# One 512-column product in place of two 256-column products in the down phases of a two-block model kernel

## What is computed

```python
# first block
h = rms_norm(x, ffn_norm_w)
x = x + (silu(h @ ffn_w_gate) * (h @ ffn_w_up)) @ ffn_w_down     # ffn_w_down: 5632 x 2048
x = rms_norm(x, final_norm_w)
# second block
h = h + mixed
h = h + conv_ffn(rms_norm_2(h, ffn_norm), ffn_w_up_2, conv_w, conv_b, ffn_w_down_2)   # ends in (...) @ w_down
return h
```

## Time and profile before

| | |
|---|---|
| median of 3 runs | 2572.27 us (2571.93, 2572.27, 2579.01) |
| profiled execution, span from first to last instruction | 2567.9 us |
| TensorE busy (matmul) | 2471.7 us, 96% of the span |
| VectorE busy | 1468.9 us, 57% |
| ScalarE busy | 1113.8 us, 43% |
| first down phase | about 1150 to 1391 us |
| second down phase | about 2320 to 2559 us |

### The profile page before, as it was taken

How to read it: one execution, slowest core, us unless ns; L and a number is a source line. 1 busy time by engine, 2 the same in 40 slices (tenths; PEclk the granted TensorE clock), 3 DMA queues, 4 the chain that set the end, 5 groups by cost and what they waited for, 6 DMA issues and landing times.

```text
span 2567.9 us, 58065 instructions
## 1 busy us (share of the span) xinstructions
PE 2471.7 (96%) x24757; PEld 2437.4 (95%) x24757; DVE 1468.9 (57%) x1657; ACT 1113.8 (43%) x1096; POOL 69.6 (3%) x70
## 2 busy tenths in 40 slices
PE   6999978989899999999998899999999999999999
PEld 6999968889899999999998899989899999999999
DVE  5457687674544544454445557674567676765444
ACT  4334434453444445443334444353455554544333
POOL 1000050001000000000100000000000000000000
PEclk8999989999999999999999999999999999999999
DMA  5555300126455555566663565535455555555664
GB/s 163 195 196 192 135 18 4 36 79 186 158 189 192 196 193 188 192 195 192 188 195 99 182 227 216 198 131 161 151 196 191 188 192 196 192 189 192 196 194 150
DMA packets 171475, 431.57 MB, mean 168 GB/s; under 512 B 17711, under 2 KB 23484, under 8 KB 170204
## 3 DMA queue, kind: packets, MB, share of 16 engines
q1 hardware_dynamic: 170123, 422.30, 50.0%
q10 hardware_dynamic: 1232, 7.52, 0.8%
HBM read 427.59 MB, written 2.17 MB: 167 GB/s over the span
## 4 chain that ended last, share of the span: by engine, by line
PE 89%; DVE 8%; ACT 2%; issue 1%; SPq 0%; DMA 0%; POOL 0%; DVEq 0%; ACTq 0%; POOLq 0%
PE ps L1813 27%; PE ps L1815 27%; PE ps L1814 27%; DVE LOW L984 1%; PE ps L1853 1%; ACT HIW L555 1%; DVE NSQ L1018 1%; PE ps L1959 1%; DVE H_ROWS L1026 0%; DVE TM L1237 0%; DVE LO L1241 0%; DVE TT L1238 0%; DVE CV L1271 0%; DVE rstd L1008 0%; DVE GT L1253 0%
## 5 line engine op out<-in xcount | busy, mean ns | idle before, releaser
L984 DVE TENSOR_TENSOR LOW<-RAW,HIW 128x2048 fp32r<-128x2048 f32 (+2 forms) x400 | 910.6, 2277 | 974.8 <-ACT HIW L555 974.8
L1813 PE MATMUL ps<-H_ROWS,HIW 128*128 128x256 f32 x4928 | 1369.6, 278 | 39.4 <-DVE LOW L984 16.9
L1814 PE MATMUL ps<-H_ROWS,HIW 128*128 128x256 f32 x4928 | 1368.6, 278 | 0.0
L1815 PE MATMUL ps<-H_ROWS,LOW 128*128 128x256 f32 x4928 | 1367.3, 277 | 0.0
L555 ACT ACTIVATE HIW<-RAW 128x2048 fp32r<-128x2048 f32 (+2 forms) x400 | 761.4, 1904 | 1178.8 <-PE ps L1815 1174.8
L1813 PEld LDWEIGHTS ps<-H_ROWS,HIW 128*128 128x128 f32 x4928 | 930.6, 189 | 43.1 <-issue 21.4
L1815 PEld LDWEIGHTS ps<-H_ROWS,LOW 128*128 128x128 f32 x4928 | 931.7, 189 | 0.0
L1814 PEld LDWEIGHTS ps<-H_ROWS,HIW 128*128 128x128 f32 x4928 | 930.5, 189 | 0.0
L1813 PE MATMUL ps<-HID,HIW 128*128 (+1 forms) x1408 | 388.7, 276 | 1.3 <-DVE LOW L984 1.3
L1815 PE MATMUL ps<-HID,LOW 128*128 (+1 forms) x1408 | 388.6, 276 | 0.0
L1814 PE MATMUL ps<-HID,HIW 128*128 (+1 forms) x1408 | 388.6, 276 | 0.0
(11 more groups left out here) (351 smaller groups left out, 1497.7 us busy)
## 6 DMA issues: line engine op xcount, KB each, us to landing
RAW<-in_ffn_w_up SPq DMA_DIRECT2D x264, 512.0 KB, 4.3
RAW<-in_ffn_w_down SPq DMA_DIRECT2D x176, 512.0 KB, 4.7
RAW<-in_w_in SPq DMA_DIRECT2D x96, 512.0 KB, 4.1
RAW<-in_fox_w_in SPq DMA_DIRECT2D x96, 512.0 KB, 4.4
RAW<-in_ffn_w_gate SPq DMA_DIRECT2D x88, 512.0 KB, 3.7
RAW<-in_w_out SPq DMA_DIRECT2D x32, 512.0 KB, 5.4
RAW<-in_fox_w_out SPq DMA_DIRECT2D x32, 512.0 KB, 4.7
INV<-rows_out ACTq DMA_DIRECT2D x4, 1024.0 KB, 7.0
```

The source lines that it names most:

```text
L984: V.tensor_tensor(LOW[:, u_const % 4, 0:n], RAW[:, u_const % 4, 0:n], HIW[:, u_const % 2, 0:n].bitcast(F32), ALU.subtract).then_inc(lo_mad ...
L1813: mm(o_, hi_w, h_hi, start=start, stop=False)
L1814: mm(o_, hi_w, h_lo, start=False, stop=False)
L1815: i = mm(o_, lo_w, h_hi, start=False, stop=stop)
```

## The change

In both down phases, and only there, the first two products of each (k, f) become one: the high weight block is loaded once and meets the 2 x 256 columns `HID[:, :, k, :]` (high part, then low part, 45,056 bytes apart in each partition), and the 512 result columns fill the whole bank `ps[f]`. The third product, low weight x high activation, is still added into columns 0 to 255. At the end of a half the two halves of each bank have to be added: `residual` first adds columns 256 to 511 to `X`, waits until that instruction has completed (`settle`), and then adds columns 0 to 255 and frees the bank. Nothing else changes; the orders of ScalarE, GpSimd and SyncE are the same.

```diff
-            def residual(m0, u_end, half):
+            def residual(m0, u_end, half, both=False):
                 for f in range(GROUP):
                     summed(m0, f, u_end)
                     x = X[:, half * 8 + f, :]
+                    if both:
+                        step(V.tensor_tensor(x, x, ps[f][:, T:2 * T], ALU.add))
+                        settle()
                     V.tensor_tensor(x, x, ps[f][:, 0:T], ALU.add).then_inc(bank_freed, 1)
...
             def down(u0, m0, last=False):
...
-                    residual(m0 + 7 * half, b + 22, half)
+                    residual(m0 + 7 * half, b + 22, half, both=True)
...
                         o_ = ps[f][:, 0:T]
-                        mm(o_, hi_w, h_hi, start=start, stop=False)
-                        mm(o_, hi_w, h_lo, start=False, stop=False)
-                        i = mm(o_, lo_w, h_hi, start=False, stop=stop)
+                        if both:
+                            mm(ps[f][:, :], hi_w, both(k), start=start, stop=False, skip_group_check=True)
+                        else:
+                            mm(o_, hi_w, h_hi, start=start, stop=False)
+                            mm(o_, hi_w, h_lo, start=False, stop=False)
+                        i = mm(o_, lo_w, h_hi, start=False, stop=stop, skip_group_check=both is not None)
...
+            def hid_both(k):
+                return HID[:, :, k, :]
```

More of the change, by code:

```diff
@@ L1793, in unit @@
             def unit(u, tiles, nf, wcol, first=False, last=False, g=None, step=0, n0=None, hcol=h_in, h_wait=None,
-                     beside=None):
+                     beside=None, both=None):
                 v = u + 1
@@ L1838, in down @@
                         unit(b + j, [2 * j, 2 * j + 1], GROUP, plain, j == 0, n0=n0 + 8 * half,
-                             hcol=lambda part, k: HID[:, part, k, :], h_wait=(S("hid_made"), made0 + 10))
+                             hcol=lambda part, k: HID[:, part, k, :], h_wait=(S("hid_made"), made0 + 10),
+                             both=hid_both)
                     with pe.Fori(0, 4) as i:
@@ L1842, in down @@
                             unit(b + 2 + j, [4 + 2 * j, 5 + 2 * j], GROUP, plain, g=i, step=4,
-                                 hcol=lambda part, k: HID[:, part, bass.ds(i * 8 + k, 1), :])
+                                 hcol=lambda part, k: HID[:, part, bass.ds(i * 8 + k, 1), :],
+                                 both=lambda k: HID[:, :, bass.ds(i * 8 + k, 1), :])
                     for j in range(18, 22):
                         unit(b + j, [2 * j, 2 * j + 1], GROUP, plain, last=j == 21,
-                             hcol=lambda part, k: HID[:, part, k, :], h_wait=(S("hid_made"), made0 + 11))
+                             hcol=lambda part, k: HID[:, part, k, :], h_wait=(S("hid_made"), made0 + 11),
+                             both=hid_both)
             def norm(k, presummed=True):
```

## The result

The changed kernel takes 2606.14 us (median of 4 runs, 2599.58 to 2610.31), the kernel before on the same occasions 2574.03 us: ratio 1.0116, 95% interval 1.0095 to 1.0137, so it is 24 to 35 us slower. The forecast was 2576.1 us with a range of 2565 to 2586. The profiled execution took 2609.17 us, its span is 2607.4 us.

The account below looks back on a forecast made before the run. Inside a half TensorE alone was taken to bound the kernel. Terms 3.7 + 2.9 + 1.5 + 3.6 + 1.4 - 9.3 = +3.8 us on a 2567.9 us span gave 2571.7, with 4.4 to the median 2576.1 us; range 2565 to 2586.

Parts of the forecast that it names:

- TensorE's term, -9.3 us: Down phases: 1408 products grow to 512 columns, each saving 6.6 ns: -9.3 us, bounds 0 and -21 us.
- I take 6.6 ns saved: Down phases: the whole 6.6 ns over the columns belongs to the instruction, so a (k, f) takes 333 ns, not 340.
- both bounds: Wide product in the down phases: 220 ns if the 6.6 ns belongs to the instruction, 226.6 if it comes with the columns.
- two runs in one instruction: Argument against the gain: the wide product reads two runs of activations, 45,056 bytes apart.
- the step of 6.7 ns from the shifted read: Argument for the gain: products reading from the shifted offset take 120 ns, so a cost of steps for each read is likelier.
- The nearest rows of plain float32: Rows used for lack of a 512-column float32r product: a 256-column record starts every 216 ns, 2.5 ns above its columns.
- The first rival: Down phases: nothing or nearly nothing gained, 0 to 2.5 ns for each (k, f): 2585.4 to 2581.9 us, slower; chance 0.25.
- The second rival: Two second halves of the down phases stay at a 117.6 ns pitch, +6.2 us: 2582.3 us, slower; chance 0.08.
- The stalls, +11.7 us: Four half ends: the doubled residual additions delay what follows by 3.7, 2.9, 1.5 and 3.6 us.
- The clock, +1.4: End of the kernel: after about 4 us idle the clock halves before or among the 32 transposes; up to 3 us, 1.4 taken.
- the faster rival: Down phases: the excess shrinks to 2.5 ns everywhere, -21 us of TensorE, sum -7.6: 2563 to 2564.7 us; chance 0.12.
- the forecast's own range: Whole kernel: 2571.5 to 2579.5 us, from stalls of 10.7 to 14.7 and 8 to 11 us gained; chance 0.48.

Follow-up runs that it names:

- column runs: Changed kernel with the activations laid out contiguously and the wide product cut to 384, 320 or 260 columns, work left out: 2528.9, 2497.2 and 2479.58 us.
- turns_wide: Changed kernel with, in the down phases except a sum's first and last k, 8 wide products to 8 banks, then 8 low products: 2596.49 us.
- contig: Changed kernel with HID laid out so that the wide product reads one contiguous run of 512 columns: 2605.03 us.
- shift64: contig with HID and what lies behind it moved by 64 bytes: 2598.52 us (single run).
- one_add: Changed kernel without the residual's first addition and its wait, TensorE work the same: 2593.34 us, 12.8 us under the changed kernel.
- before_again: The kernel before, unchanged, run for a second trace; the second half of its first down phase ran at 117.6 ns, 113.3 in the first trace.
- no_offset: The kernel before with LAST = 0 in place of 60, so the activations' last tile isn't shifted: median 2586.21 us against 2574.52, ratio 1.0035.
- before: The kernel before the change, in its first trace: 2574.03 us on the same occasions as the changed kernel.

## Why the prediction was wrong

**TensorE's term, -9.3 us: wrong in sign, +18.8 measured.** The step that failed is "I take 6.6 ns saved", with the bounds beside it: I held 220 to 226.6 ns to contain the wide product. It costs 235, outside both, and its neighbour went from 113 to 118, for which the sum had no term at all. Both bounds extrapolated one row (113.3 ns for 256 columns) by a fixed or an even price. The column runs show that the price is neither. The upper bound does hold once in each group of `turns_wide`, 226 ns for the first wide product behind fast ones; what I missed is that the stream doesn't stay at that price. Of my three arguments the runs decide two: "two runs in one instruction", held against myself, is irrelevant (`contig`), and the step of 6.7 ns from the shifted read the earlier trace rows says nothing of what a longer product pays. The nearest rows of plain float32 were also the wrong neighbours: 2.5 ns of excess there, 22 here.

By the formula of the Trainium skill, "TensorE: Matmul & The Clock Gate", section Back-to-back issue gap, a product of 512 columns would take an estimated 215.8 ns. The traces don't agree: no float32r product of 512 columns in any of them took under 224 ns, and in a steady stream its mean is 230 (`shift64`) to 235 ns (the changed kernel).

**The first rival** (nothing gained) pointed the right way but ended at 13.1 us; I had let it stop at nothing gained, when nothing in the trace excluded a loss. **The second rival** (a slower pitch that stays) was nearest in kind: the low products run at 118 ns throughout, a pair takes exactly what three products take in the slower rhythm, and the rhythm does change at stalls. I had priced it for two halves, at 4.4 ns for each of two products, on top of 9.3 us gained. For all four halves and 3 x 256 columns it comes to 1408 x 3 x 4.4 = 18.6 us; added to the first rival's 2585.4 that is 2604.0, close to what was measured. This is hindsight, and in one thing the wide kernels differ: their pair takes about 347 ns or more in every half of every trace, and not behind some stalls only. So it is likely that this is the same slowness, and not shown.

**The stalls, +11.7 us: right, in place and in size.** Measured in the changed kernel's trace: +3.6 in the middle of the first down phase (forecast 3.7). In the middle of the second, from the first addition at 2465.01 to ScalarE's release at 2474.91, 9.90 us in place of 6.66: +3.2 (2.9). End of the first, from the first addition at 1404.21 to line 1005 at 1412.33, 8.12 in place of 6.33: +1.8 (1.5). End of the kernel, first addition to first transpose, 6.44 in place of 2.86: +3.6 (3.6). **The clock, +1.4:** the fall came at the very start, 32 transposes took 6.45 us; from the first one to the end of the chain it is about 7.3 in place of 4.9, +2.4, and to the end of the span 9.8 in place of 8.4, +1.4. In sum 13.6 to 14.6 where 13.1 were booked, and `one_add`, which removes them, gained 12.8.

**The sum** with the measured terms: 18.8 + 13.6 to 14.6 = +32.4 to +33.4 us, against 32.1 between the medians. Read directly from the two traces, first to last product, the down phases last 253.4 and 251.4 us in place of 240.8 and 239.3, +24.7; with the norm's 1.8, the later transposes' 3.5 and the clock's 1.4 that is 31.4 of the profiled execution's +39.5 us. The other 8 lie outside the down phases; I estimate about 4 of them to be slow stretches such as 1759 to 1802 us, of which this trace has about 155 us and the one before 42.

Two slips in the prediction's working changed nothing: the faster rival's sum is 13.1 - 21.1 = -8.0 and not -7.6, and the forecast's own range comes to 2572.0 to 2579.0.

**What stays open** is why a product of 384 or more columns pays 21 to 22 ns where one of 256 to 320 pays 7 to 12. The jump in addresses, writes to the upper half of the bank, the bank written just before, and the activations' place beyond 7 ns are excluded. What a weight load under a long product does could not be tried apart, since each product here carries its own load; the traces show no difference in the loads themselves, which start 2 to 4 ns behind the start of the product before and have records of 188 ns in either kernel and in either rhythm (192 in part of the slow one). No version of the wide product beats the kernel before: the cheapest pair seen was 347 ns.

## What to carry to other kernels

Merging two float32r products of 256 columns into one of 512 is not a gain by itself: the columns are paid anyway, and here what was paid on top rose from 3 x 6.6 to 33 ns for each (k, f). Price a size that no row shows with a bound on the losing side too, or measure it alone first. And a doubled evacuation is paid where the stream ends, here nearly in full at three of the four half ends and by half at the fourth, where other products stood beside it, so count the boundaries before the instructions.

## What the runs showed of the hardware

- The same stream of 256-column float32r products has two stable rhythms at full clock, 113.3 and 117.6 ns. Which one follows a stall differs from execution to execution (`before_again`), and it then holds until the next stall (`no_offset`) or, it seems, until a read from a shifted start. One half of a down phase in the slow one costs 4.4 us (the first down phase lasts 245.2 us in `before_again`, 240.8 in `before`).
- A float32r product of 512 columns takes 225 to 226 ns where it is the first behind products of 256 columns at 113 ns, and 230 to 236 ns from the second one on (`turns_wide`).
- A read that starts 240 bytes further costs each product about 6.7 ns (gone in `no_offset`), and yet the kernel with the shift spreads over 9 us and the one without it over 61.
- Excess of a float32r product over its columns at 2.4 GHz: 6.6 or 11 ns at 256 columns, 11 at 260, 12 at 320, 21 at 384, 22 at 512 next to 256-column products (17 in `shift64`), 20 among its like.
